# A norm folded into the transposes of its input: a diagonal matrix in place of the scaled rows

## The reference, cut to what matters

```python
def _rmsnorm(x, g):
    xf = x.astype(jnp.float32)
    r = lax.rsqrt(jnp.mean(xf * xf, axis=-1, keepdims=True) + EPS)
    return (xf * r * g.astype(jnp.float32)).astype(x.dtype)

xn = _rmsnorm(x, g_mix[li])
proj = xn @ w_in[li]               # 1024 x 3072
# proj: u_s (512), u_p (512), gate_s (1024), gate_p (1024)
# u_s: state-space branch; u_p: pooling branch; both gated, added,
x = x + merged @ w_out[li]
x = _hmoe(x, g_ffn[li], ...)       # router, 32 experts, top 2 of 8 in one of 4 groups
return _rmsnorm(x, g_final), ...
```

## Time and profile before

| | us |
|---|---|
| median of 3 runs | 917.91 (917.82 to 918.82) |
| the profiled execution, its own time | 914.38 |
| its span, from the first to the last instruction | 912.8 |
| TensorE busy in the span | 802.4 |
| DVE busy | 263.7 |
| ACT busy | 120.0 |
| POOL busy | 128.0 |

### The profile page before, as it was taken

One profiled execution on the slowest core, in us unless ns is written; L12 is line 12 of the kernel. 1 busy time (PEld: TensorE's weight loads), 2 busy tenths in 40 slices (PEclk: granted clock), 3 DMA queues, 4 the chain that ended last, 5 costly groups with the idle time before them and its releaser, 6 DMA issues.

```text
span 912.8 us, 9587 instructions
## 1 busy us (share of the span) xinstructions
PE 802.4 (88%) x3838; PEld 455.8 (50%) x3839; DVE 263.7 (29%) x745; ACT 120.0 (13%) x230; POOL 128.0 (14%) x224
## 2 busy tenths in 40 slices
PE   2999999999999899959998788779788977988786
PEld 2788888878888655533333233323223322333332
DVE  4799756510011245461111011011101111111115
ACT  3210030120100133310000000000000000000012
POOL 3000005860033200010110001010001000100000
PEclk9999999999999999959999999889889888989998
DMA  8520221335200393367999999999999999999926
GB/s 300 142 93 16 77 105 35 110 123 188 93 1 0 116 429 153 130 255 263 426 427 427 427 428 425 428 426 427 426 426 427 427 428 427 426 427 428 391 72 253
DMA packets 41663, 251.58 MB, mean 276 GB/s; under 512 B 13061, under 2 KB 13913, under 8 KB 28786
## 3 DMA queue, kind: packets, MB, share of 16 engines
q1 hardware_dynamic: 34284, 236.97, 63.5%
q0 software_dynamic: 6672, 12.86, 4.0%
q10 hardware_dynamic: 662, 1.13, 0.4%
HBM read 245.33 MB, written 13.46 MB: 284 GB/s over the span
## 4 chain that ended last, share of the span: by engine, by line
PE 64%; DMA 31%; DVE 2%; issue 1%; ACTq 0%; ACT 0%; SPq 0%; DVEq 0%; POOLq 0%
DMA arena<-in_w_exp_up 30%; PE ps L1369 26%; PE ps L1619 14%; PE ps L1515 6%; PE ps L1632 6%; PE ps L1691 3%; PE ps L1611 1%; PE ps L1454 1%; PE ps L1449 1%; PE ps L1503 1%; PE ps L1537 1%; DVE arena L829 1%; DMA arena<-in_cache_pool 1%; PE ps L1626 1%; ACTq L588 0%
## 5 line engine op out<-in xcount | busy, mean ns | idle before, releaser
L1619 PE MATMUL ps<-arena 128*64 128x512 f32 x1024 | 255.4, 656 | 68.1 <-DMA arena<-in_w_exp_up 67.0
L1369 PE MATMUL ps<-arena 128*128 128x272 f32 x1024 | 239.0, 395 | 0.0
L1369 PEld LDWEIGHTS ps<-arena 128*128 128x128 f32 x1024 | 195.6, 192 | 39.8
L1619 PEld LDWEIGHTS ps<-arena 128*64 128x64 f32 x1024 | 86.5, 151 | 214.3 <-issue 211.9
L1632 PE MATMUL ps<-arena 128*64 128x512 f32 x512 | 116.4, 595 | 1.3 <-DVE arena L1280 1.3
L1284 DVE TENSOR_SCALAR arena<-ps,arena 128x512 f32<-128x512 f32 x32 | 24.0, 751 | 214.4 <-PE ps L1632 214.4
L782 DVE TENSOR_TENSOR arena<-arena 128x256 f32<-128x256 f32 (+10 forms) x223 | 75.5, 338 | 11.4 <-ACT arena L689 3.9
L1252 DVE TENSOR_TENSOR arena<-ps,arena 128x1024 f32<-128x1024 f32 x16 | 19.6, 1225 | 185.9 <-PE ps L1611 185.9
L1632 PEld LDWEIGHTS ps<-arena 128*64 128x64 f32 x512 | 37.8, 137 | 64.9 <-issue 61.5
L546 POOL DMA_INDIRECT y_parts<-arena x32 | 31.9, 997 | 268.0 <-DVE arena L1284 268.0
L732 ACT ACTIVATE arena<-ps,arena 128x512 f32<-128x512 f32 x32 | 22.0, 687 | 320.9 <-PE ps L1619 320.9
(11 more groups left out here) (222 smaller groups left out, 484.4 us busy)
## 6 DMA issues: line engine op xcount, KB each, us to landing
arena<-in_w_exp_gate SPq DMA_DIRECT2D x32, 2048.0 KB, 27.9
arena<-in_w_exp_up SPq DMA_DIRECT2D x32, 2048.0 KB, 32.3
arena<-in_w_exp_down SPq DMA_DIRECT2D x32, 2048.0 KB, 37.7
arena<-in_w_in SPq DMA_DIRECT2D x6, 2048.0 KB, 8.7
arena<-in_x_prompt SPq DMA_DIRECT2D x8, 512.0 KB, 6.5
arena<-in_w_out SPq DMA_DIRECT2D x2, 2048.0 KB, 10.3
arena<-y_parts SPq DMA_DIRECT2D x4, 1024.0 KB, 8.2
arena<-in_w_glu_a SPq DMA_DIRECT2D x1, 2048.0 KB, 10.7
```

Source lines behind the costliest of these rows:

```text
L1369: last = pe.matmul(dst[:, hh, 0:HALF], w[:, k, m * P:(m + 1) * P], rhs[:, k, hh * HALF:(hh + 1) * HALF], start=(k == 0), stop=(k == kk - 1))
L1619: last = pe.matmul(ps[n * TILE:(n + 1) * TILE, 2 + par, :], x_t[:, k, :], w[:, k, :], start=(k == 0), stop=(k == KD - 1))
```

## The change

The rows of x are no longer scaled before they are turned. Each tile is turned as loaded, by a plain matmul with a diagonal matrix of the inverse roots as the moving operand, and multiplied by `g_mix` when taken out of PSUM. In parts:

- DVE makes `diag` (128x128, two buffers) from `ident` with two per-row scalars: the reciprocal of the root and the Newton factor, which takes one operation less.
- DVE, and not ACT, empties xt0 to xt4, with a multiplication by `g_mix_t` (one value per partition and block, repeated over the frames). The order on DVE is scale 0, scale 1, then for each tile: take out i, scale i + 2.
- The wait for `small_in` and the copy behind it move to after scale 4.
- `g_mix` is loaded as 8 values per partition (4 KB) and not spread (512 KB).
- The blocks of channels are strided: partition p of block k holds channel 8p + k and not 128k + p. TensorE reads x with that stride as weights, and the rows of `w_in` are loaded in the same order, `(p k)` in place of `(k p)`, in pieces of 512 values as before.
- ACT has the squares and roots of the five tiles alone; root 0 now comes before square 1.

```diff
-TASKS = [(f"xt{i}", "act") for i in range(TT)] + [("par", "dve"), ("u0", "act"), ("ct", "dve")]
+TASKS = [(f"xt{i}", "dve") for i in range(TT)] + [("par", "dve"), ("u0", "act"), ("ct", "dve")]
...
-        xn_row = [at(O_XROW, D), at(O_XROW + D, D)]
+        diag = [at(O_XROW, P), at(O_XROW + P, P)]
+        g_mix_t = at(O_GB, KD)
...
-            w_in = a["w_in"][0].rearrange("(k p) (b n) -> b p k n", p=P, b=6)
+            w_in = a["w_in"][0].rearrange("(p k) (b n) -> b p k n", p=P, b=6)
...
-            load(g_b, a["g_mix"][0:1].to_broadcast((P, D)), g_in)
+            load(g_mix_t, a["g_mix"][0].rearrange("(p k) -> p k", k=KD), g_in)
...
+            def root_in(i):
+                act.wait_ge(mean_sq, i + 1)
+                act.activation(rstd[:ROWS[i], i:i + 1], ss[:ROWS[i], i:i + 1], ACT.Sqrt).then_inc(root, 1)
+
             square(0)
-            for i in range(TT):
+            root_in(0)
+            square(1)
+            for i in range(1, TT):
                 if i + 1 < TT:
                     square(i + 1)
-                act.wait_ge(mean_sq, i + 1)
-                act.activation(rstd[:ROWS[i], i:i + 1], ss[:ROWS[i], i:i + 1], ACT.Sqrt).then_inc(root, 1)
-
-            for i in range(TT):
-                psum_waits(act, f"xt{i}")
-                r = ROWS[i]
-                src = pair(NUM[f"xt{i}"]).rearrange("p h (k t) -> p (h k) t", k=4)
-                emptying(act.activation(xn_t[:, :, i * P:i * P + r], src[:, :, 0:r], ACT.Copy))
+                root_in(i)
...
-            dve.wait_ge(small_in, 16 * 9)
-            for g in range(2):
-                dve.tensor_copy(par_rows[64:80, g * N:(g + 1) * N],
-                                dt_rows[:, g:g + 1].to_broadcast((NJ, N))).then_inc(dt_ready, 1)
-            dve.wait_ge(g_in, 16)
-            for i in range(TT):
+            def scale(i):
+
                 r = ROWS[i]
                 mean, root_i = ss[:r, i:i + 1], rstd[:r, i:i + 1]
+                tmp = misc(M_SS + 16, TT)[0:r, 0:1]
                 dve.wait_ge(squares, i + 1)
                 dve.tensor_scalar(mean, mean, 1.0 / D, EPS, ALU.mult, ALU.add).then_inc(mean_sq, 1)
                 dve.wait_ge(mean_sq, i + 1)
                 dve.wait_ge(root, i + 1)
-                inverse_root(mean, root_i)
+                step(dve.reciprocal(root_i, root_i))
+                stt(tmp, root_i, mean, root_i, ALU.mult, ALU.mult)
+                ts(tmp, tmp, -0.5, ALU.mult, 1.5, ALU.add)
                 if i >= 2:
                     psum_waits(dve, f"xt{i - 2}")
-                dve.scalar_tensor_tensor(out=xn_row[i % 2][:r], in0=x_tok[:r, i, :], scalar=root_i,
-                                         in1=g_b[:r], op0=ALU.mult, op1=ALU.mult).then_inc(xn_ready, 1)
+                dve.tensor_scalar(diag[i % 2][:r], ident[:r], root_i, tmp, ALU.mult, ALU.mult).then_inc(diag_ready, 1)
+
+            def turned_in(i):
+                r = ROWS[i]
+                psum_waits(dve, f"xt{i}")
+                src = pair(NUM[f"xt{i}"]).rearrange("p h (k t) -> p (h k) t", k=4)
+                empty(dve.tensor_tensor(xn_t[:, :, i * P:i * P + r], src[:, :, 0:r],
+                                        g_mix_t.unsqueeze(2).to_broadcast((P, KD, r)), ALU.mult))
+
+            dve.wait_ge(consts, 1)
+            scale(0)
+            scale(1)
+            dve.wait_ge(g_in, 16)
+            for i in range(TT):
+                turned_in(i)
+                if i + 2 < TT:
+                    scale(i + 2)
+                if i == 2:
+                    dve.wait_ge(small_in, 16 * 9)
+                    for g in range(2):
+                        dve.tensor_copy(par_rows[64:80, g * N:(g + 1) * N],
+                                        dt_rows[:, g:g + 1].to_broadcast((NJ, N))).then_inc(dt_ready, 1)
...
-                pe.wait_ge(xn_ready, i + 1)
+                pe.wait_ge(diag_ready, i + 1)
+                blocks = x_tok[:r, i, :].rearrange("t (q k) -> t k q", k=KD)
                 for k in range(KD):
-                    last = pe.transpose(dst[:, k // 4, (k % 4) * P:(k % 4) * P + r],
-                                        xn_row[i % 2][:r, k * P:(k + 1) * P], ident[0:r, 0:r])
+                    last = pe.matmul(dst[:, k // 4, (k % 4) * P:(k % 4) * P + r], blocks[:, k, :], diag[i % 2][:r, 0:r],
+                                     start=True, stop=True)
...
-            pe.wait_ge(emptied["act"], emptied_by("act", NUM["xt4"]))
+            pe.wait_ge(emptied["dve"], emptied_by("dve", NUM["xt4"]))
```

More of the change, by code:

```diff
@@ L273, in encoder_step @@
         turned_v, scanned = sem("turned_v"), sem("scanned")
-        squares, mean_sq, root, xn_ready = sem("squares"), sem("mean_sq"), sem("root"), sem("xn_ready")
+        squares, mean_sq, root, diag_ready = sem("squares"), sem("mean_sq"), sem("root"), sem("diag_ready")
         step_dve, step_pool, ss_ready = sem("step_dve"), sem("step_pool"), sem("ss_ready")
```

## The result

The changed kernel is slower: 920.97 us median of 20 runs against 917.87 of 20 runs of the kernel before, a ratio of 1.0033 with a 95% interval of 1.002 to 1.0046. The prediction was 913.0 (910.6 to 915.4), with 0.89 on faster.

A forecast was written before the change was run, and what follows sets the result against it. TensorE, then the expert-weight stream at DMA share 0.98, bound the kernel; the first projection starting at 22.5 us instead of 27.4 saves 4.9 us, taking the median 917.91 to 913.0, range 910.6 to 915.4.

The forecast's parts named there:

- The bound and where the gain would come from: TensorE, then the expert-weight stream, set the pace; the first projection's start decides: 22.5 us for 27.4, 4.9 sooner.
- what was taken off DVE's front: The small-load wait leaves the front of DVE's queue, so DVE begins tile 0 at 8.6 us, not 12.07.
- the sum: Chain through DVE's scales and take-outs and TensorE's turns: first projection begins at 22.5 us, 4.9 us sooner.
- the first projection would take 9.3 us again: Sign in the next profile: first 32 instructions of L1369 at 9.3 us, still at the slow rate.
- `w_in` in its new order: Loading w_in rows in new order costs nothing; first block, landed at 18.1 us, is wanted at 22.5.
- A plain matmul in place of a transpose: TensorE's 40 turn matmuls: taken at the transposes' 1.94 us per tile, at most 2.3, fitting in 2.6.
- one of the signs of being wrong that the prediction named: In the next profile, TensorE turns longer than 2.3 us would show the forecast wrong.
- the stride is not new: Strided weights in the turns: the experts' turn (L1611) already reads so, eight in 1.99 us, then 1.09.
- The rival on the other side: At L1352 the turns become the bound and the kernel gets slower, about 930 us; chance 0.04.
- the formula 10.0 + 0.7 + 0.9 + 36.2 p: First projection's start if turns bound, p us per plain matmul; meets 27.4 at p = 0.44.
- The fast rate sooner: Plain matmuls bring TensorE's fast rate sooner, first projection takes 7.34 us: 911.0 us; chance 0.15.
- its p of 0.98: Slow-rate price per plain matmul if four times a transpose: first projection at 47.1, 937.6 us.

The follow-up runs named there:

- run 1: The changed kernel with its 40 plain matmuls made transposes with the unit matrix, the inverse-root scaling left out: 912.77 us, ratio 0.9955.
- run 6: The changed kernel with contiguous channel blocks, w_in in its old order and g_mix as 1024 single values: 911.75 us, ratio 0.9946.
- runs 2: The kernel before with only its 40 transposes made plain matmuls with the unit matrix: 916.96 us, ratio 1.0003.
- run 5: The changed kernel with nine extra matmuls of 512 columns on TensorE ahead of the turns: 922.07 us, ratio 1.0051.
- run 9: The changed kernel with contiguous channel blocks and eight extra matmuls of 512 columns ahead of the turns: 913.54 us, ratio 0.9944.

## Why the prediction was wrong, point by point

**The bound and where the gain would come from: right.** The start of the first projection decides, with how long it takes (the table above); what was taken off DVE's front came in full (8.59 for its first mean, 8.6 forecast), and with transposes in place the sum came out at 21.79 against 22.5 (run 1). That the first projection would take 9.3 us again did not hold: it took 10.47 in the changed kernel, and from 7.60 to 10.23 in the runs. `w_in` in its new order landed at 3.29 + 12.6 = 15.9 us in the changed kernel, sooner than before, and was waited for by nobody.

**The step that failed: "A plain matmul in place of a transpose".** It put a tile's turn at 1.94 us, at most 2.3, so that it would fit into DVE's period; it measured 3.9 us, and the turns became the bound. That was one of the signs of being wrong that the prediction named. The step had two errors.

First, 0.58 / 4 = 0.145 us was taken for a plain matmul, from four rows of L1449. They are two matmuls:

```python
for g in range(2):
    pe.matmul(dst[0:NC, g, o], usq[...], toep[...], start=True, stop=False)
```

In the same way the 16 matmuls of a `project` stand as 32 rows, and the 8 transposes of a turn as 8: in these kernels a plain float32 matmul is two matrix instructions, a transpose is one. The code beside the count of rows would have shown that. The price of a plain 128-column matmul at the slow rate is 0.49 in the changed kernel, and some 0.43 on contiguous weights (in run 6 17 loads start from 10.5 to 13.9), and not the 0.24 to 0.29 of the forecast. Without the stride it costs part of the gain: in run 6 the first two turns are held up and the last takes 1.94 us for 1.06, and the first projection comes at 24.61 and not at 21.79 as in run 1 (0.5 of that is a later start, with the first mean at 8.93 for 8.41).

Second, "the stride is not new" took the strided reading from transposes (L1611). At the fast rate an instruction takes, by rows and runs:

| weights | transpose | plain |
|---|---|---|
| contiguous | 3.64 / 32 = 0.114 (L1404 before) | 2.05 / 16 = 0.128 (runs 2, 6) |
| stride 32 bytes | 1.09 / 8 = 0.136 | 19.21 / 80 = 0.240 (run 5) |

The contiguous transposes are these:

```profile
119.77 3.64 PE ps L1404 x32
```

Only the lower right corner is dear. Of the two kernels compared only the changed one has it, and its weight loads say so. In the changed kernel, and then in run 6 (count, ns least/median/most):

```profile
L1372 PEld LDWEIGHTS ps<-arena x80: 307/336/340, 10.2 to 29.2; 128*128 128x128 f32 x64, 32*128 32x128 f32 x16
```

```profile
L1372 PEld LDWEIGHTS ps<-arena x80: 181/192/338, 10.5 to 23.8; 128*128 128x128 f32 x64, 32*128 32x128 f32 x16
```

With the stride the loads stay near 336 ns, whereas in run 6 they fall from some 333 ns to 192 once the rate is there. So the stride costs little at the slow rate, and at the fast rate it keeps the loads as slow as before; rows of a stage at the slow rate could hardly have shown its price. With contiguous weights a turn of 2 x 8 x 0.128 = 2.05 us fits into DVE's period; with strided ones 3.9 does not, at either rate.

**The rival on the other side** had this mechanism and the formula 10.0 + 0.7 + 0.9 + 36.2 p, with the point p = 0.49 from which slower could be told. The price measured is 0.486, which gives 29.2; 30.47 came. The formula took the fifth tile at half a turn, but its 16 instructions cost 3.9 us, as much as those of a full tile (its loads of 128 columns took 329 ns in the mean, the others 336). That adds 1.85; the other terms came to 11.0 and not 11.6. The rival's chance of 0.04 rested on the misread 0.145, and its price of about 930 us was too high: 3.1 us were lost.

**The fast rate sooner.** By the Trainium skill (TensorE: Matmul & The Clock Gate, Part 4: PE-mode transpose) the full clock does not engage for transposes. Run 1 disagrees: with transposes alone the fourth turn takes 1.16 us after three of some 1.94, and only behind it does the granted clock fall to 0.50 (from 19.8 us on). The first projection at 7.60 came in runs 2 and 6, with plain matmuls on contiguous weights, but not in run 9 with the same (9.29); the changed kernel's plain ones kept TensorE without a gap, and the granted clock still fell to 0.50 behind them. The forecast had put this rival at 0.15, and nothing here shows what decides it.

The Trainium skill (same page, Terms) says that the transpose mode is four times faster for FP32. The trace gives 2 x 0.128 / 0.114 = 2.2 with contiguous weights, and 2 x 0.240 / 0.136 = 3.5 with strided ones. The prediction put that rule aside by the misread row. With that rule its p of 0.98 would have been twice the measured 0.486.

What stays open: why the fast rate came in one execution's first projection and not in another's, and why L1594 took 3.66 or some 5 us. No run varied that alone. Why the stride costs a plain matmul so much more than a transpose isn't shown either, only that it does.

## What to carry to other kernels

Before a row is used as the price of an operation, divide its count by the number of calls in the code: here a plain float32 matmul is two instructions and a transpose one. A layout that costs transposes little can cost plain matmuls much; read the duration of the weight loads, and keep plain float32 weights contiguous or at a stride of 8 bytes at most. When a fold moves a scaling into a matmul, keep the blocks contiguous, if the small load can be had in that order: run 6 loads `g_mix` as 1024 single values and `w_in` as before, 911.75 us against 918.19, ratio 0.9946.

## What the runs showed of the hardware that was not expected

- At the fast rate a plain float32 load of 128 columns took 192 ns contiguous and 336 ns at a stride of 32 bytes (runs 6 and 5); per instruction 0.128, 0.134 (8 bytes), 0.238 (16 bytes), 0.240 to 0.243 (32 bytes) us. A transpose with the same 32 byte stride took 0.136.
- TensorE without a gap for 19.4 us in strided loads was granted a clock of 0.50 at their end (29.6 to 35 us). In run 6, with gaps and contiguous loads, it stayed 1.00 through the first projection, but in run 9, with gaps and contiguous loads too, it was 0.59 from 24 to 28 us. So neither the gaps nor the stride explain the falls.
- The loads of the 32-row tile cost as much as those of 128 rows: 16 instructions in 1.94 us (run 6), against 2.05.
